# The triangular inverses of the RWKV mix: four merge levels on 32x32 blocks, and a fifth that makes only the blocks off the diagonal

## The reference, cut to what matters

```python
def step(state, inp):
    r_t, w_t, k_t, v_t, kk_t, a_t = inp
    sa = jnp.einsum('bhvk,bhk->bhv', state, -kk_t)
    state = (state * w_t[:, :, None, :]
             + sa[..., None] * (kk_t * a_t)[:, :, None, :]
             + v_t[..., None] * k_t[:, :, None, :])
    return state, jnp.einsum('bhvk,bhk->bhv', state, r_t)
_, y = lax.scan(step, state0, (r, w_h, k, v, kk, a_h))   # 256 tokens
```

## Time and profile before

| | |
|---|---|
| median of 3 runs | 1037.79 us (1037.22 to 1041.79) |
| profiled execution: its time | 1040.44 us |
| profiled execution: its span | 1038.5 us |
| mean granted clock in it | 0.977 |
| PE, DVE, ACT busy | 962.8, 671.3, 545.8 us |
| the merge levels, start of `first` to the end of level 5 | 297.8 to 348.7 us of the span |

### The profile page before, as it was taken

The page is one execution under the profiler, slowest core; times in us unless marked ns, Lnnn a source line. Parts: engine busy times, 40 slices in busy tenths (PEclk is TensorE's granted clock), DMA queues, the critical chain, the costliest instruction groups (busy, mean ns, idle before and its releaser), DMA issues.

```text
span 1038.5 us, 17402 instructions
## 1 busy us (share of the span) xinstructions
PE 962.8 (93%) x6074; PEld 816.8 (79%) x6074; DVE 671.3 (65%) x1103; ACT 545.8 (53%) x987; POOL 26.7 (3%) x53
## 2 busy tenths in 40 slices
PE   6999999989767999999999997898999899999997
PEld 5788888867567977888888786787888777888885
DVE  4776666756875346776666676687546456766664
ACT  5655555575624425655555564645736546554552
POOL 3002000000000000000000000000200000000000
PEclk9999999989899999999999998999899999999999
DMA  6777666453311013776666745454035146665661
GB/s 197 220 220 216 198 187 192 131 141 102 98 46 44 3 32 101 213 211 189 185 184 198 214 136 148 119 175 153 2 102 173 51 127 184 199 198 185 181 197 64
DMA packets 204832, 153.60 MB, mean 148 GB/s; under 512 B 5947, under 2 KB 190624, under 8 KB 204784
## 3 DMA queue, kind: packets, MB, share of 16 engines
q1 hardware_dynamic: 203760, 151.35, 48.9%
q0 software_dynamic: 1024, 1.61, 0.6%
HBM read 151.89 MB, written 1.05 MB: 147 GB/s over the span
## 4 chain that ended last, share of the span: by engine, by line
PE 77%; DVE 10%; ACT 6%; issue 3%; DMA 3%; SPq 0%; DVEq 0%; ACTq 0%
PE ps L473 76%; DVE wlo L1523 2%; ACT whi L1100 2%; DMA raw<-in_w_ckv 1%; ACT XT L1136 1%; ACT arena L1121 1%; PE ps L547 1%; DVE XT L1568 1%; DMA raw<-in_w_co 1%; DMA X<-in_x 0%; DVE X L1542 0%; ACT arena L1268 0%; DVE arena L1668 0%; DVE arena L1769 0%; DVE arena L1797 0%
## 5 line engine op out<-in xcount | busy, mean ns | idle before, releaser
L473 PE MATMUL ps<-XT,whi 128*128 128x512 f32 x1440 | 524.7, 406 | 8.7 <-DVE XT L1568 6.7
L1523 DVE TENSOR_TENSOR wlo<-raw,whi 128x1024 fp32r<-128x1024 f32 x280 | 337.1, 1223 | 132.1 <-ACT whi L1100 111.3
L473 PE MATMUL ps<-XT,wlo 128*128 128x256 f32 x1440 | 406.7, 282 | 0.0
L473 PEld LDWEIGHTS ps<-XT,whi 128*128 128x128 f32 x1440 | 273.8, 190 | 77.5 <-issue 6.3
L1100 ACT ACTIVATE whi<-raw 128x1024 fp32r<-128x1024 f32 x280 | 293.3, 1055 | 62.2 <-PE ps L473 21.1
L473 PEld LDWEIGHTS ps<-XT,wlo 128*128 128x128 f32 x1440 | 275.2, 191 | 3.9 <-issue 0.5
L473 PE MATMUL ps<-whi,H 128*128 128x512 f32 x608 | 178.0, 393 | 3.9 <-issue 2.5
L473 PEld LDWEIGHTS ps<-whi,H 128*128 128x128 f32 x608 | 109.0, 188 | 27.8 <-issue 3.6
L473 PE MATMUL ps<-arena 64*64 64x64 f32 (+6 forms) x1576 | 101.0, 253 | 13.5 <-DVE arena L1789 4.2
L473 PEld LDWEIGHTS ps<-arena 64*64 64x64 f32 (+3 forms) x1576 | 92.7, 156 | 21.4 <-DVE arena L1789 4.6
L473 PE MATMUL ps<-wlo,H 128*128 128x512 f32 x304 | 95.7, 393 | 0.0
(11 more groups left out here) (246 smaller groups left out, 711.0 us busy)
## 6 DMA issues: line engine op xcount, KB each, us to landing
raw<-in_ffn_w_gate SPq DMA_DIRECT2D x44, 512.0 KB, 4.6
raw<-in_ffn_w_up SPq DMA_DIRECT2D x44, 512.0 KB, 3.9
raw<-in_ffn_w_down SPq DMA_DIRECT2D x44, 512.0 KB, 4.7
raw<-in_w_in SPq DMA_DIRECT2D x36, 512.0 KB, 3.9
raw<-in_w_up SPq DMA_DIRECT2D x32, 512.0 KB, 4.6
raw<-in_w_down SPq DMA_DIRECT2D x32, 512.0 KB, 3.5
raw<-in_w_out SPq DMA_DIRECT2D x16, 512.0 KB, 3.4
raw<-in_w_ckv SPq DMA_DIRECT2D x16, 512.0 KB, 4.6
```

What stands on the lines that cost most here:

```text
L473: return pe.matmul(o, st, mv, start=start, stop=stop, skip_group_check=True)
L1523: dve.tensor_tensor(wlo[:, n % RING, :], raw[:, n % RAW, :], whi[:, n % RING, :].bitcast(F32), sub).then_inc(lo_ready, 1)
```

## The change

The blocks on the diagonal are held as 32x32 blocks, four in a column of partitions (`QUARTERS`), in place of 64x64 blocks, two in a column. `XY` is half as wide: 128 columns for an inverse and 128 for its transpose. Levels 1 to 4 work on 32x32 blocks; each step has twice as many matmuls as before, of 32x32 by 32 columns, and its copies are half as wide. `tiles` now goes through the four quarters of one group, then of the other.

Level 5 joins two 32x32 blocks to one of 64x64. Since the blocks on the diagonal are known, it makes only those off it (`joints`, `joined`): 16 matmuls in `corrections(5, p)`, which now multiply across the quarters, and 24 in `joined`: 8 for the inverse, in one quarter only, since only the first 64 rows are read later, and 16 for the transposes. The known blocks have to be copied to where they are read: ACT copies them after level 4 into a new buffer `X64` (two instructions, semaphore `x_diag`), and after level 5 into `YZ` (eight, `y_diag`). The parts of `YZ` and `X64` that are zero are cleared by POOL: seven memsets in place of two.

```diff
-        XY = ar(1024 * 8, NF, 2 * T)
+        XY = ar(1024 * 8, NF, T)
+        X64 = ar(1024 * 9, NF, T)
@@ PE
-                    one, two = PAIRS[p]
-                    for first_rows, second_rows in ((TOP, BOTTOM), (BOTTOM, TOP)):
-                        for m in range(4):
-                            yield one, m, first_rows
-                            yield two, m, second_rows
+                    for m in range(4):
+                        for f in PAIRS[p]:
+                            for rows in QUARTERS:
+                                yield f, m, rows
+
+                def joints(p):
+
+                    for m in range(4):
+                        for f in PAIRS[p]:
+                            for h in range(2):
+                                yield f, m, QUARTERS[2 * h], QUARTERS[2 * h + 1]
...
+                    if k < 5:
+                        for f, m, rows in tiles(p):
+                            ms = slice(32 * m, 32 * m + 32)
+                            last = mm(PS[2 * f][rows, ms], ULK[rows, f, m // 2, m % 2, rows], XY[rows, f, ms])
+                    else:
+                        for f, m, early, late in joints(p):
+                            ms = slice(32 * m, 32 * m + 32)
+                            last = mm(PS[2 * f][late, ms], ULK[early, f, m // 2, m % 2, late], XY[early, f, ms])
...
+                def joined(p):
+
+                    pe.wait_ge(t_ev, 4 * 4 + 2 * p + 2)
+                    for f, m, early, late in joints(p):
+                        ms, ys = slice(32 * m, 32 * m + 32), slice(P + 32 * m, P + 32 * m + 32)
+                        if late == QUARTERS[1]:
+                            mm(PS[2 * f + 1][late, ms], XY[late, f, ys], TP[late, f, ms])
+                    for f, m, early, late in joints(p):
+                        ms, ys = slice(32 * m, 32 * m + 32), slice(P + 32 * m, P + 32 * m + 32)
+                        last = mm(PS[2 * f + 1][early, ys], TP[late, f, ms], XY[late, f, ys])
+                    last.then_inc(xy_mm, 1)
...
                 pe.wait_ge(xy_ev, 20)
+                pe.wait_ge(x_diag, 2)
...
                 pe.wait_ge(yf_ev, 4)
+                pe.wait_ge(y_diag, 8)
@@ ACT
-                                act.activation(XY[:, f, :], PS[2 * f + 1][:, :], ACT.Copy).then_inc(xy_ev, 1)
+                                act.activation(XY[:, f, :], PS[2 * f + 1][:, 0:T], ACT.Copy).then_inc(xy_ev, 1)
                             else:
-                                act.activation(YZ[f // 2][TOP, 4 * (f % 2):4 * (f % 2) + 4, TOP],
-                                               four(PS[2 * f + 1][TOP, T:2 * T]), ACT.Copy)
-                                act.activation(XY[TOP, f, 0:T], PS[2 * f + 1][TOP, 0:T], ACT.Copy).then_inc(xy_ev, 1)
+                                late = QUARTERS[1]
+                                act.activation(four(X64[late, f, :])[:, :, 0:32], four(PS[2 * f + 1][late, 0:P]),
+                                               ACT.Copy).then_inc(xy_ev, 1)
+                    if k == 4:
+                        act.wait_ge(xy_ev, 16)
+                        act.wait_ge(yf_zero, 7)
+                        for q in range(2):
+                            rows = QUARTERS[q]
+                            act.activation(X64[rows, :, :].rearrange("p f (m s) -> p f m s", m=4)[:, :, :, 32 * q:32 * q + 32],
+                                           XY[rows, :, 0:P].rearrange("p f (m s) -> p f m s", m=4), ACT.Copy).then_inc(x_diag, 1)
+                    if k == 5:
+                        for g in range(2):
+                            for rows in QUARTERS:
+                                act.activation(YZ[g][rows, :, rows].rearrange("p (f m) s -> p f m s", f=2),
+                                               XY[rows, 2 * g:2 * g + 2, P:T].rearrange("p f (m s) -> p f m s", m=4),
+                                               ACT.Copy).then_inc(y_diag, 1)
@@ DVE
-                    for rows in (TOP, BOTTOM):
+                    for rows in QUARTERS:
...
-                        dve.tensor_tensor(four(TP[:, f, :]), four(PS[2 * f][:, 0:T]), bc(con(f"step{k}"), 4),
-                                          mul).then_inc(t_ev, 1)
+                        if k < 5:
+                            dve.tensor_tensor(four(TP[:, f, 0:P]), four(PS[2 * f][:, 0:P]), bc(con(f"step{k}"), 4),
+                                              mul).then_inc(t_ev, 1)
+                        else:
+                            dve.tensor_copy(TP[:, f, 0:P], PS[2 * f][:, 0:P]).then_inc(t_ev, 1)
@@ POOL
-            for g in range(2):
-                pool.memset(YZ[g][BOTTOM, :, TOP], 0.0).then_inc(yf_zero, 1)
+            zeroed = [X64[QUARTERS[0], :, :]] + [YZ[g][r, :, c] for g in range(2) for r, c in
+                      ((BOTTOM, TOP), (QUARTERS[1], QUARTERS[0]), (QUARTERS[3], QUARTERS[2]))]
+            for n, part in enumerate(zeroed):
+                pool.memset(part, 0.0).then_inc(yf_zero, 1)
+                pool.wait_ge(yf_zero, n + 1)
```

More of the change, by code:

```diff
@@ L74 @@
 for _name, _n in [("ident", P), ("eps", 1), ("eps_block", 1), ("eps_group", 1), ("swap32", P), ("swap64", P), ("blk", P), ("lt", P), ("le", P),
-                  ("first", P // 2)] + [(f"step{k}", P // 2) for k in range(1, 6)] + \
+                  ("first", P // 4)] + [(f"step{k}", P // 4) for k in range(1, 5)] + \
                  [("prev", P), ("diag", P), ("invc", 4 * PAD), ("freq", 1), ("sign", 1),
@@ L98, in constants @@
     put("le", i <= j)
-    half = np.arange(P // 2)
-    for k in range(6):
-        pair = (half[:, None] >> (k + 1)) == (half[None] >> (k + 1))
-        lower = pair & (((half[:, None] >> k) & 1) == 1) & (((half[None] >> k) & 1) == 0)
-        unit = half[:, None] == half[None]
-        put(f"step{k}" if k else "first", np.tile(unit | (lower if k else lower.T), (2, 1)))
+    at = np.arange(P // 4)
+    for k in range(5):
+        pair = (at[:, None] >> (k + 1)) == (at[None] >> (k + 1))
+        lower = pair & (((at[:, None] >> k) & 1) == 1) & (((at[None] >> k) & 1) == 0)
+        unit = at[:, None] == at[None]
+        put(f"step{k}" if k else "first", np.tile(unit | (lower if k else lower.T), (4, 1)))
     put("prev", np.where(j > i, 0.0, NEG))
@@ L374, in build @@
         TOP, BOTTOM = slice(0, 64), slice(64, 128)
+        QUARTERS = [slice(32 * q, 32 * q + 32) for q in range(4)]
         ORDER = list(range(6, 12)) + list(range(6))
@@ L658, in first @@
                     for m in range(4):
-                        ms = slice(64 * m, 64 * m + 64)
-                        for rows in (TOP, BOTTOM):
-                            last = mm(PS[2 * f][rows, ms], XY[rows, f, T + 64 * m:T + 64 * m + 64], ident[rows, rows])
+                        ms, ys = slice(32 * m, 32 * m + 32), slice(P + 32 * m, P + 32 * m + 32)
+                        for rows in QUARTERS:
+                            last = mm(PS[2 * f][rows, ms], XY[rows, f, ys], ident[rows, rows])
                     last.then_inc(x1_mm, 1)
@@ L685, in corrections @@
                             pe.wait_ge(xy_ev, 4 * (k - 2) + 2 * p + i + 1)
-                    for f, m, rows in tiles(p):
-                        ms = slice(64 * m, 64 * m + 64)
-                        last = mm(PS[2 * f][rows, ms], ULK[rows, f, m // 2, m % 2, rows], XY[rows, f, ms])
+                    if k < 5:
[6 more added lines that the diff above has]
+                            last = mm(PS[2 * f][late, ms], ULK[early, f, m // 2, m % 2, late], XY[early, f, ms])
                     last.then_inc(t_mm, 1)
@@ L723, in mix @@
                         last = mm(PS[4 + 2 * (f // 2)][BOTTOM, (f % 2) * T + 64 * m:(f % 2) * T + 64 * m + 64],
-                                  ULK[TOP, f, m // 2, m % 2, BOTTOM], XY[TOP, f, ms])
+                                  ULK[TOP, f, m // 2, m % 2, BOTTOM], X64[TOP, f, ms])
                     if f % 2:
@@ L1261, in mix @@
                         act.wait_ge(x1_mm, n + 1)
-                        act.activation(XY[:, f, 0:T], PS[2 * f][:, 0:T], ACT.Copy).then_inc(x1_ev, 1)
+                        act.activation(XY[:, f, 0:P], PS[2 * f][:, 0:P], ACT.Copy).then_inc(x1_ev, 1)
                     for i in range(2):
@@ L1775, in strict @@
                     a = CONST_COLS["first"][0]
-                    for rows in (TOP, BOTTOM):
-                        y = XY[rows, f, T:2 * T].rearrange("p (h c s) -> p h c s", h=2, c=2)
-                        mask = CON[rows, a:a + 64].rearrange("p (a b c) -> p a b c", a=1, b=1).broadcast_to([64, 2, 2, 64])
+                    for rows in QUARTERS:
+                        y = XY[rows, f, P:T].rearrange("p (h c s) -> p h c s", h=2, c=2)
+                        mask = CON[rows, a:a + 32].rearrange("p (a b c) -> p a b c", a=1, b=1).broadcast_to([32, 2, 2, 32])
                         ins = dve.tensor_tensor(y, ULK[rows, f, :, 0:2, rows], mask, mul)
-                        if rows is TOP:
+                        if rows is QUARTERS[3]:
```

(10 more changed lines are left out.)

15 lines of the change are left out of this document (9 added, 6 removed).

## The result

| | before | changed |
|---|---|---|
| median of the runs | 1039.29 us (4 runs, 1037.22 to 1041.79) | 1054.79 us (4 runs, 1052.52 to 1055.35) |
| profiled execution: time, span | 1040.44, 1038.5 us | 1054.87, 1052.9 us |
| mean granted clock | 0.977 | 0.947 |

The change makes the kernel slower by 1.44%: the ratio is 1.0144, with a 95% interval from 1.0113 to 1.0174. That is about 15 us, where I had forecast 3 us less.

What follows compares the result with a forecast made beforehand. PE was taken as the bound, with DVE in levels 2 and 3. Chain shifts of +0.64, −0.74, −1.10 and −3.96 us, then −2.96 after the wait behind level 5, gave 1037.79 − 3.0 = 1034.8 us; range 1031.5 to 1049.

Steps and rivals of the forecast that it cites:

- a packet still comes faster than it is used: PE's instruction queue: packets take 1.2 us each, one used up in 1.9 us instead of 3.7, so supply costs nothing.
- the price of 15 ns: PE's levels: each record of 32 columns costs 15 ns, where one of 64 columns costs 29.2.
- the rival's 1053.8 us: PE's levels: a 32-column record costs the full 29.2 ns, +16.0 us; a price over 26 had 13%.
- a price above 22.7 ns: PE's levels: 32-column records cost more than 22.7 ns, the price that gives +5.2 us; chance 29%.
- all four quarters overlap: PE's levels: records at 7.5 ns, PE waits for DVE and ACT, 1031.7 us; 11% together with larger gains at waits.
- The price of 25 ns: PE's levels: the skill's floor from start to start for small matmuls, giving +9.0 us, or 1046.8.
- My reason against it: PE's levels: a matmul's second record waits for its first, holds up what follows, and keeps the overlap at two.
- The line from 57.8 and 29.2 through the columns: PE's record prices at 128 and 64 columns, extended to 32 columns: 14.9 ns, taken as 15.
- First inverses: Ahead of level 1: longer `strict`, shorter `corrected`, small change in `first` and `corrections`; PE's row at 314.31 shifts by +0.64 us.
- Levels 1 to 4: PE's shift goes from +0.64 to −1.10 us, through shorter copies and a vanished wait; DVE bounds levels 2 and 3.
- Level 5 and behind: Level 5 gains 2.86 us; behind it PE waits about 1.0 us before `y12` for ACT's eight copies.
- a fall of the clock: PE's levels: use in 32x32 pieces drops the clock to 1.2 GHz, records cost 30 ns, near 1054 us; chance 3%.

Runs made afterwards that it cites:

- the last loop kernel: 32x32 kernel with levels 2 to 4 as a hardware loop, DVE's better order, ACT's eight copies moved behind level 4, plus 16 long records in level 5: 1039.10 us.
- the loop: Changed kernel with PE's levels 2 to 4 as three passes over one body, plus four additional matmuls per pass: 1040.64 us, ratio to before 1.0040.
- the fifth level alone: Kernel before with levels 1 to 4 on 64x64 blocks and only level 5's off-diagonal 32x32 blocks made: 1037.28 us, ratio 0.9993.

## Why the prediction was wrong

The forecast was −3.0 us, the result +15. The step that failed is the one with which I put the instructions' supply at nothing: "a packet still comes faster than it is used". It doesn't. A packet came in 3.80 us, 29.7 ns a record, while PE could use one up in 1.1 us at full clock and 1.9 at half. So the price of 15 ns, on which all hangs, was not what the levels paid. That the rival's 1053.8 us, from 29.2 ns, lies within 1 us of the result is luck: that was the array's price of a larger record, and the supply's interval happens to be nearly the same. I gave a price above 22.7 ns 29%, and the range ended at 1049. Point by point:

1. *The price.* What the array takes depends on how many quarters come in turn. With four, as in levels 1 to 4, it is 8.4 ns at full clock and 13.3 at half. With two, as in level 5's corrections, 15: in the last loop kernel 32 of them take 0.69 us at full clock, less the tail of 0.21. So 15 was right for level 5, and for the other levels nearly twice too high; the rival "all four quarters overlap" was right about the array. The price of 25 ns that I gave as another rival isn't seen for quarters in turn. My reason against it, that a matmul's second record holds up what is behind it, isn't borne out. One bank for all four quarters didn't prevent the 8.4 ns; whether four banks would do better wasn't run. The line from 57.8 and 29.2 through the columns was a weak reading, since both kinds of columns, moving and stationary, had changed together in my two rows, and the run with halved moving columns didn't follow it. None of this sets the pace here. PE gets a record every 29.7 ns, since 256 instructions come in 3.8 us.
2. *The supply of instructions.* I had it in the rival: packets of 16 KB, 1.2 us each, one used up in 1.9 us instead of 3.7. I then judged it by the time that a packet takes (1.2 us, less than 1.9) and not by the interval at which packets come. In the kernel before most packets come 4 us and more apart; the two that come closest begin at 316.46 and 319.86 us, 3.4 apart. I should have taken that as the fastest rate seen, 27 ns a record, and it would have said "slower". The kernel before stood, unnoticed, right at the edge: 29.2 ns a record from the array, 29.7 from the supply. The Trainium skill ("Runtime: NRT & Kernel Launch", Instruction fetch mechanics) says that crossing a 16 KiB boundary is mostly hidden; the trace disagrees for these small matmuls, with 1.5 to 2.1 us of idle at each from 328.68 us on.
3. *First inverses.* Forecast +0.64, measured +1.28. The masked products of 32x128 took 1.23 us for four (forecast 1.16), `corrected` 0.49 (0.48). The other 0.6 is the clock: it fell at 303 us instead of 308.8, and the products of `outward` took 3.79 instead of 3.17 us.
4. *Levels 1 to 4.* Forecast −1.7 from there, and DVE as the bound of levels 2 and 3. The shorter copies are as forecast (ACT's pairs 0.66, DVE's 0.49), but DVE and ACT now wait for PE, so they gain nothing. The share of PE's busy time that I read as 92 to 97% is 90 in one of the stretches (6.09 of 6.80 us).
5. *Level 5 and behind.* The two copies to `X64` took 1.28 us (1.3) and were hidden, the eight to `YZ` 3.48 us (3.4). The 1.0 us that I charged for them did not fall due: PE's pooled matmuls took 1.8 us longer at half clock, and ACT was done first. In the run with long matmuls, where they ran at full clock, 0.81 us of it did.
6. *The clock.* I gave a fall of the clock 3% and argued that it was at 1.00 in every stretch with 64x64 pieces. The same trace has a stretch at 0.74, just ahead of those in the earlier trace rows and behind PE's idle time of 3.22 us; its row stands below. In the changed kernel it fell, and cost about 1.8 + 0.6 + 0.4 = 2.8 us outside the levels. In the levels it cost next to nothing, as the run with long matmuls in the idle times shows: at a clock of 0.74 the records came no faster.

```profile
310.00:314.30 4.30, 3.03 (x32) 2.86 (x33) 0.00 (x0) 2.53 (x5) 0.98 (x2) 0.74 0.00 0
```

The likely division of the 15 us is then: 12.4 from the levels, 2.8 from the clock outside, 0.6 from `strict`, less what came back later. Of the 12.4, the loop took away 10.6, which is what is shown for the supply; the rest is a likely share of it, since the loop's first pass and level 1 still wait.

What stays open: why a packet comes only every 3.8 us when its transfer takes 1.15; that the next one is asked for only when the one before is in use would explain it and fits the times at which the transfers begin, but no run tests this. Nor do the runs show what lets the clock fall in the kernels without gaps.

## What to carry to other kernels

Where PE runs many small matmuls that are written out, count its instructions. Here 256 of them, 128 matmul records with their weight loads, came once in 3.8 us over a long stretch, and never sooner than 3.4 us after the last (319.14 to 322.52 us in the loop kernel), and beyond that rate a smaller or better overlapping tile gained nothing. Judge a supply by the interval at which it comes, and not by the time that one transfer takes. The sign in a timeline is idle time that "issue" ends, at every 128 records, wherever the steps begin. A hardware loop removed it here, with a body of 48 KB. The 64x64 matmuls, at 29.2 ns a record, were already at that rate. And look for two engines that are idle one after the other: the swap of two steps on DVE, seen on the way, was worth more than the fifth level alone.

## What the runs showed of the hardware

- The supply of PE's instructions: 3.80 us a packet of 256 over seven packets (29.7 ns a record with its weight load), all at half clock. At full clock two pieces began 3.57 and 3.84 us ahead of the next. A loop body of 48 KB ran its second and third pass without any packet.
- Records of 32x32 by 32 columns, in one bank: with four quarters in turn 8.4 ns each at full clock and 13.3 at half, with two in turn 15 at full clock. Records of 64x64 in two halves in turn: 29.2 ns by 64 columns, and 29.4 by 32 with twice as many in a row in each half.
- The clock was at 0.51 for 101 us while PE was busy for 100.78 of them, with records of 64x64 by 32; so a busy PE in the profile is no sign of a full clock. Four long records (128x128 by 256 columns) in a wait went with a clock of 1.00 in level 5, where it was 0.67 without them, and with them 1.6 us of the matmuls behind it. In the changed kernel, 22 of them between 330 and 360 us brought it from 0.50 to 0.74 only.
